# Two thirds of a modulation product: from the first stage into prompt attention

## The chip, the cores and the metric

One core of a Trainium2 chip runs the whole program. The time is device microseconds of one execution; the figure of a kernel is the median over its runs. "The trace" is one profiled execution of the kernel before, with a start and a duration for every instruction and transfer, counted in microseconds from the start of its span.

Engines are named as the profile names them: PE multiplies matrices, PEld loads its weights, DVE and ACT are the vector and the scalar engine, POOL is GpSimd, SP only issues transfers. A line such as "SPq" is the instruction queue of SP.

## The reference, cut to what matters

```python
def _decoder_layer(x, c, conv_prefix, attend, layer_idx, p):
    shift1, scale1, gate1, shift2, scale2, gate2 = _adaln(c, p['w_ada'], p['b_ada'])  # silu(c) @ w_ada + b_ada
    h = x * (1 + scale1) + shift1
    proj = h @ p['w_in']                       # q, k, v, B, C, u
    ...
    o_att = _diff_post(attend(q, k, v, lam), p['subln_w'], lam_init)
    o_conv, conv_state = _short_conv(gb, gc, hc, conv_prefix, p['conv_w'])
    mix = jnp.concatenate([o_att, o_conv], axis=-1) @ p['w_out']
    x = _layer_norm(DEEPNORM_ALPHA * x + gate1 * mix, p['ln1_g'], p['ln1_b'])
    h2 = x * (1 + scale2) + shift2
    f = _peer(h2.reshape(b * s, d), ...).reshape(b, s, d)
    x = _layer_norm(DEEPNORM_ALPHA * x + gate2 * f, p['ln2_g'], p['ln2_b'])
```

The layer runs for a prompt (1024 tokens, one row of c) and for a sample group (8 sequences of 4 tokens, eight rows of c) with the same weights. `w_ada` is 1024 x 6144 floats, 25 MB: six vectors of 1024 for each of the nine rows of c. `shift1` and `scale1` are wanted by the projection; `gate1`, `shift2`, `scale2` and `gate2` only after attention.

## The kernel before

`build` runs six stages one after another, each closed by a barrier of all engines (`end_stage`): `condition` (modulation, bias tables), `project` (q, k, v, then `conv`), `prompt_attention`, `sample_attention` (paged cache), `mix` (output product, first layer norm) and `peer` (expert retrieval, 1056 indirect gathers, by far the longest).

**condition.** SP loads `w_ada` in 12 blocks of 512 columns (2 MB each, L201) into four slots, then the three parts of `w_qkv` that the next stage multiplies (2 MB each, L204). PE multiplies each block as it lands: 32 matmuls with 128 columns (L257), each of which the trace shows as two instructions, so 64 for a block. After four blocks DVE adds the bias (L303) into `mod`. The first four blocks are shift1 and scale1; they alone are turned into `modT`. When all twelve are done, SP stores `mod` to DRAM with four transfers (`mod_scratch`, L207), waits for them (L208) and for `w_qkv` (L209). `mix` reads the last four vectors from that scratch.

**prompt_attention.** There are 32 units k, eight tiles t of 128 queries by four heads h; unit k has (k // 4 + 1) * 128 keys. `heads` sets one fixed order on each engine: in turn k PE does `scores` of unit k+3 (L665), `turn` of unit k+1 (transposes of the weights, L673) and `values` of unit k (L682); DVE does `combined` of unit k+1 (L709 to L716) and `biased` of unit k+3 (bias and row maximum, L698 to L702); ACT does the exponentials of unit k+2 (L730), the copy of the turned weights of unit k+1 (L737) and, after the last head of a tile, the copy of the output (L744). The scores have one set of PSUM banks: `scores` of the next unit waits until `biased` has read the last. The output banks alternate by tile (6 and 7). SP loads the four bias strips (576 KB each, L641), for all of which DVE waits before its first unit, and then issues the 18 stores of the convolution's state (L645, L647), 512 elements of 4 bytes each, and waits for them before the barrier.

Of the kernel before, what the change touches and what calls it, by code (L numbers as in the profile page):

```python
# [99 lines left out]
def build(nc, A):  # L100
    with ExitStack() as top:
# [28 lines left out]
        with ExitStack() as mid:  # L130
            pre = ExitStack()
            tensors |= dict(pre=pre, w_qkv=sbuf(pre, "w_qkv", [P, KD, 3 * AW], side="right"))
            tensors["modT"] = sbuf(mid, "modT", [P, 2, KD, NC])
            condition(**tensors)
# [20 lines left out]
def condition(nc, A, sem, sbuf, psum, mod_dram, toep_dram, ident, ones, modT, lam, eps, w_qkv, **_):  # L155

    NBLK, SL, G = 12, 4, 4  # L160
    with ExitStack() as st:
        w = sbuf(st, "w_ada", [P, SL, KD, BANK])
# [4 lines left out]
        cT = sbuf(st, "cT", [P, KD, NS])  # L167
        lq = sbuf(st, "lq", [1, 4, DH])
# [9 lines left out]
        consts, b_land, b_zero = sem("consts"), sem("b_ada_land"), sem("b_ada_zero")  # L178
        w_land, w_free = ([sem(f"w_ada_{what}{u}") for u in range(SL)] for what in ("land", "free"))
        qkv_land, mod_first = sem("w_qkv_land"), sem("mod_first")  # L180
        silu, cT_psum, cT_sbuf = sem("silu"), sem("cT_psum"), sem("cT_sbuf")
        m_psum, m_free = [sem(f"m_psum{u}") for u in range(2)], [sem(f"m_free{u}") for u in range(2)]
        mod_ready, modT_psum, lam_exp, lam_arg, lam_bc, lam_row = (sem("mod_ready"), sem("modT_psum"), sem("lam_exp"),
                                                                  sem("lam_arg"), sem("lam_bc"), sem("lam_row"))
        dve_c, act_c, ones_ready, mod_stored = sem("dve_c"), sem("act_c"), sem("ones_ready"), sem("mod_stored")
# [3 lines left out]
        mod_v = mod_dram.rearrange("c (n j x) -> c n j x", j=G, x=P)  # L189
        with nc.Block() as block:  # L190
            @block.sync
            def _(sp):
                sp.dma_start(rel[0:BUCKETS, :], A["rel_bias"]).then_inc(rel_land, 16)
                sp.dma_start(hot[:], A["const_onehot"]).then_inc(rel_land, 16)
                sp.dma_start(c[0:1, :], A["c_prompt"]).then_inc(consts, 16)
                sp.dma_start(c[1:NC, :], A["c_sample"]).then_inc(consts, 16)
                sp.dma_start(ident[:], A["const_ident"]).then_inc(consts, 16)
                for n in range(NBLK):
                    if n >= SL:
                        sp.wait_ge(w_free[n % SL], n // SL)  # L200
                    sp.dma_start(w[:, n % SL], w_v[:, :, n * BANK:(n + 1) * BANK]).then_inc(w_land[n % SL], 16)  # L201
                for j in range(3):
                    cols = slice(j * AW, (j + 1) * AW)
                    sp.dma_start(w_qkv[:, :, cols], wq_v[:, :, cols]).then_inc(qkv_land, 16)  # L204
                sp.wait_ge(mod_ready, 1)
                for j in range(G):
                    sp.dma_start(mod_v[:, :, j, :], mod[j * NS:j * NS + NC]).then_inc(mod_stored, 16)  # L207
                sp.wait_ge(mod_stored, 16 * G)  # L208
                sp.wait_ge(qkv_land, 16 * 3)  # L209

            @block.scalar
            def _(act):
# [3 lines left out]
                for j in range(G):  # L216
                    act.dma_start(b4[j * NS:j * NS + NC], b_v[:, :, j, :].to_broadcast([NC, NBLK, P])).then_inc(b_land, 16)
                act.wait_ge(consts, 7 * 16)
# [11 lines left out]
            def _(pe):  # L230
# [18 lines left out]
                for n in range(NBLK):  # L249
                    u, m, at = n % SL, (n // G) % 2, (n % G) * P  # L250
                    pe.wait_ge(w_land[u], 16 * (n // SL + 1))
                    if n == 2 * G:
                        pe.wait_ge(m_free[m], 1)
                    for k in range(KD):
                        for j in range(G):

                            ins = nc.tensor.matmul(psum[j * NS:(j + 1) * NS, m, at:at + P], cT[:, k, :], w[:, u, k, j * P:(j + 1) * P],  # L257
                                                   start=(k == 0), stop=(k == KD - 1), skip_group_check=True)
                    ins.then_inc(w_free[u], 1)
                    if n % G == G - 1:  # L260

                        pe.wait_ge(w_free[u], n // SL + 1)
                        pe.sem_inc(m_psum[m], 1)

# [8 lines left out]
            def _(dve):  # L273
# [26 lines left out]
                dve.wait_ge(b_land, 16 * G)  # L300
                for q in range(NBLK // G):
                    dve.wait_ge(m_psum[q % 2], q // 2 + 1)
                    step(nc.vector.tensor_tensor(mod[:, q * G:(q + 1) * G, :].rearrange("p n x -> p (n x)"), psum[:, q % 2, :],  # L303
                                                 b4[:, q * G:(q + 1) * G, :].rearrange("p n x -> p (n x)"), ALU.add))
                    step.tell(m_free[q % 2], *([mod_first] if q == 0 else []))
                step.tell(mod_ready)
                dve.wait_ge(modT_psum, 1)
# [300 lines left out]

def prompt_attention(nc, A, sem, sbuf, psum, toep_dram, ident, ones, lam, qT, kT, v, o_att, zlast, zslast, **_):

# [4 lines left out]
    with ExitStack() as st:  # L615
# [5 lines left out]
        mx, nmx, z = (sbuf(st, n, [P, 3, 2]) for n in ("row_max", "neg_max", "row_sum"))  # L621
        rz = sbuf(st, "row_scale", [P, 2])
        T = {n: sem("at_" + n) for n in
             "s_ready s_free e_ready p_ready w_ready w_free wT_psum wT_free wT_ready o_ready o_free".split()}
        dve_c, act_c, strip_land, state_stored = sem("at_dve"), sem("at_act"), sem("at_strip"), sem("at_state_stored")

        def heads(*parts):


            for k in range(-3, TILES * H):  # L630
                for ahead, part in parts:
                    if 0 <= k + ahead < TILES * H:
                        part(k + ahead, (k + ahead) // H, (k + ahead) % H)

        with nc.Block() as block:
            @block.sync
            def _(sp):
                for h in range(H):

                    f = toep_dram[h].rearrange("q m -> (q m)")[P - 1:P - 1 + P * (TOEP - 1)]  # L640
                    sp.dma_start(strip[:, h, :], f.rearrange("(q m) -> q m", q=P)[:, 0:STRIP]).then_inc(strip_land, 16)  # L641

                with nc.allow_non_contiguous_dma("small"):
                    for r in range(2):
# [4 lines left out]
                sp.wait_ge(state_stored, 16 * 2 * (1 + NB))  # L649

            @block.tensor
            def _(pe):
                pe.sem_inc(T["s_free"], 1)
                pe.sem_inc(T["w_free"], 1)
                pe.sem_inc(T["wT_free"], 1)
                pe.sem_inc(T["o_free"], 2)

# [31 lines left out]
            def _(dve):  # L689
# [15 lines left out]
                def combined(k, t, h):  # L705
# [13 lines left out]
                    step.reset()  # L719
                heads((1, combined), (3, biased))  # L720

            @block.scalar
            def _(act):
# [17 lines left out]
                def output(k, t, h):  # L741
                    if h == H - 1:
                        take(act, T["o_ready"])
                        step(nc.scalar.copy(o_att[:, t, :], psum[:, 6 + t % 2, :]))  # L744
                        step.tell(T["o_free"])
                        step.reset()
# [1202 lines left out]
```

## Time and profile before

| | us |
|---|---|
| median of 3 runs | 3984.93 |
| lowest and highest of the 3 | 3982.57, 3989.07 |
| the profiled execution | 3991.51 |
| its span in the trace | 3989.5 |
| first stage, in the trace | 0 to about 95 |
| prompt attention, in the trace | about 480 to 649 |

The page of the profile gives for the whole span PE 60% busy, DVE 64%, ACT 37%, POOL 33%, and the DMA engines at nine tenths or more in 29 of the 40 slices, most of them in `peer`. Since the stages are closed by barriers, a stage's length is set by whatever ends last inside it, and its rows have to be read by themselves.

### The profile page before, as it was taken

How to read it: one execution, taken by the hardware profiler on the slowest of the kernel's cores; microseconds unless marked ns; L12 is line 12 of the kernel's file. 1: busy time of each engine (PE TensorE's matmuls, PEld its weight loads, DVE VectorE, ACT ScalarE, POOL GpSimd, SP SyncE). 2: the span in 40 equal slices, each digit the busy share in tenths (PEclk: the TensorE clock that was granted, in tenths of full speed). 3: DMA queues.
4: the chain of work that ended last, by engine and by line, in shares of the span. 5: the costliest groups of instructions: out<-in, count | busy, mean ns of one | idle time of the engine just before them, and what ended most of it. 6: DMA issues, size and time to landing. Idle time of an engine off the chain costs nothing. (4 is left out here: it accounts for less than half of the span.)

```text
span 3989.5 us, 55293 instructions
## 1 busy us (share of the span) xinstructions
PE 2409.4 (60%) x16678; PEld 1084.2 (27%) x16678; DVE 2542.6 (64%) x6416; ACT 1465.6 (37%) x4223; POOL 1296.8 (33%) x1334
## 2 busy tenths in 40 slices
PE   5999776898765354553564465465356456446543
PEld 3446445565322121220121121122112112112110
DVE  1111165666475888677677677767757767767775
ACT  0110053333003455543434444444444344444443
POOL 0000001444002344443444344444344444444442
PEclk7999978999887565775675676566567567657655
DMA  9102134999328899999999999999999999999998
GB/s 359 49 33 61 24 1 144 407 411 387 138 92 315 353 396 404 421 420 421 411 417 413 419 415 418 403 421 412 421 407 418 419 406 420 421 420 414 419 412 333
DMA packets 245932, 1343.89 MB, mean 337 GB/s; under 512 B 47288, under 2 KB 60825, under 8 KB 94084
## 3 DMA queue, kind: packets, MB, share of 16 engines
q0 software_dynamic: 164352, 1174.49, 71.4%
q1 hardware_dynamic: 64072, 147.14, 10.9%
q10 hardware_dynamic: 17212, 18.74, 1.4%
q8 instruction: 133, 2.18, 0.2%
q14 instruction: 163, 1.34, 0.1%
HBM read 1319.30 MB, written 20.97 MB: 336 GB/s over the span
## 5 line engine op out<-in xcount | busy, mean ns | idle before, releaser
L1595 PE MATMUL psum<-sb_ring,sb_fold_weighted 128*32 128x256 f32 x8448 | 1008.9, 569 | 1307.6 <-PEq L62 1203.0
L1563 POOL DMA_INDIRECT sb_ring<-in_uv,sb_experts x1056 | 1151.4, 1090 | 1655.6 <-POOLq L62 1504.6
L1780 DVE CUSTOM_DVE_ANT_0 sb_ring<-sb_ring,sb_h_four 128x1024 f32<-128x1024 f32 x1056 | 1265.8, 1225 | 652.6 <-DMA sb_ring<-in_uv,sb_experts 615.4
L1595 PEld LDWEIGHTS psum<-sb_ring,sb_fold_weighted 128*32 128x32 f32 x8448 | 268.6, 134 | 2012.8 <-issue 2003.2
L1685 ACT ACTIVATE sb_gelu<-sb_dots 128x1 f32<-128x1 f32 x1056 | 210.3, 199 | 994.4 <-ACTq L62 985.8
L806 POOL DMA_DIRECT2D sb_v_pages<-in_cache_v x256 | 135.0, 527 | 861.5 <-issue 683.5
L1690 ACT ACTIVATE sb_fold_weighted<-sb_fold,sb_expert_w 128x32 f32<-128x32 f32 x1056 | 339.3, 321 | 34.4
L1618 PE MATMUL psum<-sb_w_pq,sb_h2T 128*128 128x512 f32 x576 | 336.6, 738 | 1.5 <-issue 1.5
L1687 ACT ACTIVATE sb_expert_w<-sb_gelu,sb_gates 128x1 f32<-128x1 f32 x1056 | 311.1, 295 | 34.5
L1664 ACT COPY sb_h_four<-sb_h_tiles 32x1024 f32<-32x1024 f32 x180 | 187.5, 1042 | 4.2
L1618 PEld LDWEIGHTS psum<-sb_w_pq,sb_h2T 128*128 128x128 f32 x576 | 132.4, 242 | 193.4 <-issue 193.4
L541 PE MATMUL psum<-sb_hT,sb_w_bcu 128*128 128x352 f32 x576 | 172.3, 462 | 8.4 <-PEq L62 8.4
L386 PE MATMUL psum<-sb_w_qkv,sb_hT_tile 128*128 128x512 f32 x384 | 168.0, 597 | 0.0
L849 PE MATMUL psum<-sb_ident,sb_k_pages 128*128 128x128 f32 x1024 | 127.6, 279 | 42.3 <-DMA sb_k_pages<-in_cache_k 24.9
L849 PEld LDWEIGHTS psum<-sb_ident,sb_k_pages 128*128 128x128 f32 x1024 | 113.7, 143 | 58.5 <-DMA sb_k_pages<-in_cache_k 37.8
L541 PEld LDWEIGHTS psum<-sb_hT,sb_w_bcu 128*128 128x128 f32 x576 | 110.3, 192 | 69.9 <-issue 9.7
L950 ACT COPY sb_k_pagesT<-psum 128x512 f32<-128x512 f32 x128 | 74.2, 587 | 107.3 <-PE psum L849 104.1
L1030 DVE COPY sb_k_pagesT<-psum 128x512 f32<-128x512 f32 x128 | 86.1, 689 | 43.0 <-PE psum L849 39.5
L466 DVE TENSOR_SCALAR sb_hT_tile<-psum,sb_modT 128x128 f32<-128x128 f32 x64 | 21.1, 405 | 135.7 <-DVEq L62 135.7
L1734 ACT COPY sb_queries<-psum 128x512 f32<-128x512 f32 x36 | 21.1, 586 | 208.9 <-ACTq L62 208.9
L386 PEld LDWEIGHTS psum<-sb_w_qkv,sb_hT_tile 128*128 128x128 f32 x384 | 73.1, 192 | 89.2 <-issue 89.1
L1793 DVE MAX8 sb_sv<-sb_scores_pk 128x8 f32<-128x128 f32 x288 | 69.9, 285 | 32.1 <-DVEq L62 29.5
(227 smaller groups left out, 2646.7 us busy)
## 6 DMA issues: line engine op xcount, KB each, us to landing
sb_k_pages<-in_cache_k SPq DMA_DIRECT2D x256, 256.0 KB, 6.1
sb_v_pages<-in_cache_v POOLq DMA_DIRECT2D x256, 256.0 KB, 6.2
sb_w_ada<-in_w_ada SPq DMA_DIRECT2D x12, 2048.0 KB, 17.0
sb_ring<-in_uv,sb_experts POOLq DMA_INDIRECT x1056
sb_w_qkv<-in_w_in SPq DMA_DIRECT2D x3, 2048.0 KB, 19.3
sb_w_bcu<-in_w_in SPq DMA_DIRECT2D x12, 512.0 KB, 6.3
sb_w_pq<-in_w_pq SPq DMA_DIRECT2D x3, 2048.0 KB, 17.1
sb_h_tiles<-h_scratch SPq DMA_DIRECT2D x9, 512.0 KB, 9.2
```

The source lines that it names most:

```text
L386: ins = nc.tensor.matmul(psum[0:n, 2 + j, :], hTt[:, u, k, 0:n], w[:, k, j * AW:(j + 1) * AW], start=(k == 0), stop=(k == KD - 1))
L541: ins = nc.tensor.matmul(where(u, part, j), w[:, u, j, k, :], hT[:, k, at:at + n], start=(k == 0), stop=(k == KD - 1))
L806: eng.dma_start(slots[g::CH, u, :, :].rearrange("q j n -> q (j n)"), cache[ds(page, 1)].rearrange("a (q j) n -> (a q) (j n)", j=CH))\
L849: ins = nc.tensor.transpose(psum[:, KT + h, j * P:(j + 1) * P], kp[:, u, j, h * P:(h + 1) * P], ident[:])
L1563: pool.indirect_dma_start(ring[:, slot, :], None, uv, bass.IndirectOffsetOnAxis(ap=experts[:, u, g, n:n + 1], axis=0))\
L1595: ins = nc.tensor.matmul(psum[q * NS:(q + 1) * NS, bank, at:at + QUARTER], fw[:, slot, :], ring[:, slot, D + q * QUARTER:D + (q + 1) * QUA ...
L1618: ins = nc.tensor.matmul(psum[:, 4 + n % 2, :], hT[:, k, :], w[:, k, n * BANK:(n + 1) * BANK], start=(k == 0), stop=(k == KD - 1), skip_gr ...
L1664: step(nc.scalar.copy(h2x[q * NS:(q + 1) * NS, half, :], h2[g * NS:(g + 1) * NS, u, :]))
L1685: step(nc.scalar.activation(act_g[:, slot:slot + 1], dots[:, slot:slot + 1], ACT.Gelu))
L1687: step(nc.scalar.activation(wgt[:, slot:slot + 1], act_g[:, slot:slot + 1], ACT.Copy, scale=gates[:, u, g, n:n + 1]))
L1690: nc.scalar.activation(fw[:, slot, :], fold[:, 0:NS], ACT.Copy, scale=wgt[:, slot:slot + 1]).then_inc(T["diag_ready"], 1)
L1780: dot = nc.vector.tensor_tensor_reduce(ring[:, slot, 0:D], ring[:, slot, 0:D], h2x[:, half], 1.0, 0.0, ALU.mult, ALU.add, dots[:, slot:slo ...
```

## The change

Blocks 4 to 11 of `w_ada` leave `condition`. In `prompt_attention` they come back as 16 pieces of 1 MB (half the depth of a block, two slots), loaded by SP behind the strips and the bias rows, and multiplied by PE behind `values` in turns 2 to 9 and 12 to 19, with 16 matmuls a piece. DVE adds each pile of four blocks to the bias in turns 10 and 20. The store to `mod_scratch` now stands in this stage, and the state stores stand behind it in SP's queue. PE's product takes PSUM bank 7, so the output banks no longer alternate. `cT` moves to a buffer that lives longer. POOL clears the 128 x 1024 tile `mod_late` before SP loads the bias rows into it.

```diff
@@ condition
-    NBLK, SL, G = 12, 4, 4
+    NBLK, G = 4, 4
...
                 for n in range(NBLK):
-                    if n >= SL:
-                        sp.wait_ge(w_free[n % SL], n // SL)
-                    sp.dma_start(w[:, n % SL], w_v[:, :, n * BANK:(n + 1) * BANK]).then_inc(w_land[n % SL], 16)
+                    sp.dma_start(w[:, n], w_v[:, :, n * BANK:(n + 1) * BANK]).then_inc(w_land[n], 16)
...
-                sp.wait_ge(mod_ready, 1)
-                for j in range(G):
-                    sp.dma_start(mod_v[:, :, j, :], mod[j * NS:j * NS + NC]).then_inc(mod_stored, 16)
-                sp.wait_ge(mod_stored, 16 * G)
                 sp.wait_ge(qkv_land, 16 * 3)
@@ prompt_attention
+        w_ada = sbuf(st, "w_ada_late", [P, 2, HALF, BANK])
+        mod = sbuf(st, "mod_late", [P, NBLK, P])
...
+        OUT, MOD = 6, 7
+        def modulation(k):
+            if 2 <= k < 2 + NBLK:
+                return k - 2
+            if 12 <= k < 12 + NBLK:
+                return k - 12 + NBLK
+            return None
@@ block.sync, behind the four strips
+                sp.wait_ge(mod_zero, 1)
+                for j in range(G):
+                    sp.dma_start(mod[j * NS:j * NS + NC], b_v[:, G:G + NBLK, j, :].to_broadcast([NC, NBLK, P])).then_inc(b_land, 16)
+                for i in range(2 * NBLK):
+                    u, n, half = i % 2, i // 2, i % 2
+                    if i >= 2:
+                        sp.wait_ge(w_free[u], n)
+                    sp.dma_start(w_ada[:, u], w_v[:, half * HALF:(half + 1) * HALF, (G + n) * BANK:(G + n + 1) * BANK]).then_inc(w_land[u], 16)
+                sp.wait_ge(mod_ready, PILES)
+                for j in range(G):
+                    sp.dma_start(mod_v[:, G:G + NBLK, j, :], mod[j * NS:j * NS + NC]).then_inc(mod_stored, 16)
+                sp.wait_ge(mod_stored, 16 * G)
                 with nc.allow_non_contiguous_dma("small"):
@@ block.tensor
-                        ins = nc.tensor.matmul(psum[:, 6 + t % 2, h * DV:(h + 1) * DV], wT[:, k % 2, j, :],
+                        ins = nc.tensor.matmul(psum[:, OUT, h * DV:(h + 1) * DV], wT[:, k % 2, j, :],
...
+                def modulate(k, t, h):
+                    i = modulation(k)
+                    if i is None:
+                        return
+                    u, n, half = i % 2, i // 2, i % 2
+                    if i == NBLK:
+                        pe.wait_ge(mod_ready, 1)
+                    pe.wait_ge(w_land[u], 16 * (n + 1))
+                    for c in range(HALF):
+                        for g in range(G):
+                            ins = nc.tensor.matmul(psum[g * NS:(g + 1) * NS, MOD, n % G * P:(n % G + 1) * P], cT[:, half * HALF + c, :],
+                                                   w_ada[:, u, c, g * P:(g + 1) * P], ...)
+                    ins.then_inc(w_free[u], 1)
+                    if (i + 1) % NBLK == 0:
+                        pe.wait_ge(w_free[u], n + 1)
+                        pe.sem_inc(m_psum, 1)
-                heads((3, scores), (1, turn), (0, values))
+                heads((3, scores), (1, turn), (0, values), (0, modulate))
@@ block.vector
+                def modulated(k, t, h):
+                    if k not in (10, 20):
+                        return
+                    pile = (k - 10) // 10
+                    dve.wait_ge(m_psum, pile + 1)
+                    dve.wait_ge(b_land, 16 * G)
+                    part = mod[:, pile * G:(pile + 1) * G, :].rearrange("p n x -> p (n x)")
+                    step(nc.vector.tensor_tensor(part, psum[:, MOD, :], part, ALU.add))
+                    step.tell(mod_ready)
-                heads((1, combined), (3, biased))
+                heads((1, combined), (3, biased), (0, modulated))
```

The order on SP in the first stage and in prompt attention, before (`x12` and the like count transfers of one form; `sb_z_last` and `sb_z_sample_last` are the convolution's state):

```order
L201 DMA sb_w_ada<-in_w_ada 128x8x512 x12
L204 DMA sb_w_qkv<-in_w_in 128x8x512 x3
L207 DMA mod_scratch<-sb_mod 108x1x128 x4
...
L641 DMA sb_bias_strip<-toep_scratch 128x1152 x4
L645 DMA out_new_conv_prompt<-sb_z_last 128x4x1
L647 DMA out_new_conv_sample<-sb_z_sample_last 128x4x1 x8
```

and with the change:

```order
L198 DMA sb_w_ada<-in_w_ada 128x8x512 x4
L201 DMA sb_w_qkv<-in_w_in 128x8x512 x3
...
L644 DMA sb_bias_strip<-toep_scratch 128x1152 x4
L648 DMA sb_mod_late<-in_b_ada 9x8x128 x4
L653 DMA sb_w_ada_late<-in_w_ada 128x4x512 x16
L656 DMA mod_scratch<-sb_mod_late 9x8x128 x4
L660 DMA out_new_conv_prompt<-sb_z_last 128x4x1
```

Eight blocks and the store of `mod` have gone from the first stage, and 24 transfers stand between the strips and the first state store.

The order on PE in prompt attention, turns 2 and 3 without the `scores` that open turn 2, before:

```order
L673 MATMUL psum<-sb_ident,sb_weights 128x128
L682 MATMUL psum<-sb_v,sb_weightsT 128x128
L665 MATMUL psum<-sb_kT,sb_qT 128x256 x2
L673 MATMUL psum<-sb_ident,sb_weights 128x128 x2
L682 MATMUL psum<-sb_v,sb_weightsT 128x128
```

and with the change:

```order
L692 MATMUL psum<-sb_ident,sb_weights 128x128
L701 MATMUL psum<-sb_v,sb_weightsT 128x128
L716 MATMUL psum<-sb_w_ada_late,sb_cT 32x128 x16
L684 MATMUL psum<-sb_kT,sb_qT 128x256 x2
L692 MATMUL psum<-sb_ident,sb_weights 128x128 x2
L701 MATMUL psum<-sb_v,sb_weightsT 128x128
L716 MATMUL psum<-sb_w_ada_late,sb_cT 32x128 x16
```

A piece of 16 matmuls, and the wait for its landing ahead of it, now stands between `values` and the next `scores`.

## Rows read from the trace of the kernel before

**Rows 1.** Engines' busy time by stretch, first stage: columns in the first line.
```profile
core 0: us, PE busy (x) PEld busy (x) DVE busy (x) ACT busy (x) POOL busy (x), PEclk, DMA share, GB/s
0.00:95.00 95.00, 53.34 (x806) 38.03 (x806) 11.47 (x23) 4.05 (x5) 0.20 (x4) 0.79 0.98 367
```

**Rows 2.** Timeline of PE, `w_ada` blocks: start, duration, what, [idle before, its releaser].
```profile
36.14 3.64 PE L257 MATMUL psum<-sb_w_ada,sb_cT 128*32 128x128 f32 x64 [2.91 <-DMA sb_w_ada<-in_w_ada]
...
46.38 1.95 PE L257 MATMUL psum<-sb_w_ada,sb_cT 128*32 128x128 f32 x64 [1.49 <-DMA sb_w_ada<-in_w_ada]
...
77.14 1.95 PE L257 MATMUL psum<-sb_w_ada,sb_cT 128*32 128x128 f32 x64 [2.02 <-DMA sb_w_ada<-in_w_ada]
```

**Rows 3.** End of the first stage: SP's issues, then SP's waits (total, times, longest).
```profile
80.14 7.13 SPq L207 DMA_DIRECT2D mod_scratch<-sb_mod  x4
95.77 0.99 SPq L355 DMA_DIRECT2D sb_x_in<-in_x_prompt  x2
...
SPq L209 <- DMA sb_w_qkv<-in_w_in: 6.0, 1, 6.0
...
SPq L190 <- DMA mod_scratch<-sb_mod: 1.0, 1, 1.0
```

**Rows 4.** Start of prompt attention: timeline, the strips' landing, then stretches (columns of rows 1).
```profile
480.47 2.13 SPq L641 DMA_DIRECT2D sb_bias_strip<-toep_scratch  x4
...
483.12 18.59 SPq L647 DMA_DIRECT2D out_new_conv_sample<-sb_z_sample_last  x8
499.02 0.29 DVE L698 CUSTOM_DVE_ANT_0 sb_scores<-psum,sb_bias_strip 128x128 f32<-128x128 f32 x1 [19.76 <-DVEq L62]
...
DMA to landing us min/median/max: 3.8/6.0/16.7
...
480.00:490.00 10.00, 0.80 (x4) 0.54 (x4) 0.00 (x0) 0.00 (x0) 0.00 (x0) 0.50 0.79 237
490.00:499.00 9.00, 0.00 (x0) 0.00 (x0) 0.00 (x0) 0.00 (x0) 0.00 (x0) 0.50 0.52 1
```

**Rows 5.** Issue to landing of the 512 KB loads of `w_bcu`, issued in threes.
```profile
DMA to landing us min/median/max: 3.9/6.3/9.3
```

**Rows 6.** Timeline of PE, one turn with 384 keys at the low clock.
```profile
528.73 1.65 PE L665 MATMUL psum<-sb_kT,sb_qT 64*128 64x384 f32 x4 [0.65 <-PEq L62]
...
530.75 0.88 PE L673 MATMUL psum<-sb_ident,sb_weights 128*128 128x128 f32 x3 [0.37 <-PEq L62]
...
531.42 1.06 PE L682 MATMUL psum<-sb_v,sb_weightsT 128*128 128x128 f32 x4
...
532.41 1.65 PE L665 MATMUL psum<-sb_kT,sb_qT 64*128 64x384 f32 x4
```

**Rows 7.** Timeline of PE, one turn with 512 keys at the high clock.
```profile
543.76 1.13 PE L665 MATMUL psum<-sb_kT,sb_qT 64*128 64x512 f32 x4 [0.68 <-PEq L62]
...
545.98 0.63 PE L673 MATMUL psum<-sb_ident,sb_weights 128*128 128x128 f32 x4 [1.09 <-PEq L62]
...
546.45 0.83 PE L682 MATMUL psum<-sb_v,sb_weightsT 128*128 128x128 f32 x6
...
547.85 1.13 PE L665 MATMUL psum<-sb_kT,sb_qT 64*128 64x512 f32 x4 [0.57 <-PEq L62]
```

**Rows 8.** PE alone, a stretch of early units: length, busy, granted clock, DMA share, GB/s.
```profile
509.00:519.00 10.00, 7.32 (x26) 0.50 1.43 2
```

**Rows 9.** Timeline of DVE: the addition of a pile of four blocks.
```profile
40.02 0.69 DVE L303 TENSOR_TENSOR sb_mod<-psum,sb_b_ada 128x512 f32<-128x512 f32 x1 [12.68 <-PEq L263]
```

**Rows 10.** State stores' last issues and SP's wait; end of DVE's turn 20; last output copy.
```profile
503.43 16.70 SPq L647 DMA_DIRECT2D out_new_conv_sample<-sb_z_sample_last  x8
...
SPq L635 <- DMA out_new_conv_sample<-sb_z_sample_last: 16.1, 1, 16.1
...
589.92 0.17 DVE L702 TENSOR_SCALAR sb_neg_max<-sb_row_max 128x2 f32<-128x2 f32 x1
...
647.80 0.59 ACT L744 COPY sb_o_att<-psum 128x512 f32<-128x512 f32 x1 [2.49 <-ACTq L62]
```

More of the change, by code:

```diff
@@ L133, in build @@
             tensors["modT"] = sbuf(mid, "modT", [P, 2, KD, NC])
+            tensors["cT"] = sbuf(mid, "cT", [P, KD, NS])
             condition(**tensors)
@@ L152, in build, with condition @@
         peer(**tensors)
-def condition(nc, A, sem, sbuf, psum, mod_dram, toep_dram, ident, ones, modT, lam, eps, w_qkv, **_):
-    NBLK, SL, G = 12, 4, 4
+def condition(nc, A, sem, sbuf, psum, toep_dram, ident, ones, modT, cT, lam, eps, w_qkv, **_):
+    NBLK, G = 4, 4
     with ExitStack() as st:
-        w = sbuf(st, "w_ada", [P, SL, KD, BANK])
+        w = sbuf(st, "w_ada", [P, NBLK, KD, BANK])
         b4 = sbuf(st, "b_ada", [P, NBLK, P])
@@ L178, in condition @@
         consts, b_land, b_zero = sem("consts"), sem("b_ada_land"), sem("b_ada_zero")
-        w_land, w_free = ([sem(f"w_ada_{what}{u}") for u in range(SL)] for what in ("land", "free"))
+        w_land = [sem(f"w_ada_land{n}") for n in range(NBLK)]
         qkv_land, mod_first = sem("w_qkv_land"), sem("mod_first")
         silu, cT_psum, cT_sbuf = sem("silu"), sem("cT_psum"), sem("cT_sbuf")
-        m_psum, m_free = [sem(f"m_psum{u}") for u in range(2)], [sem(f"m_free{u}") for u in range(2)]
-        mod_ready, modT_psum, lam_exp, lam_arg, lam_bc, lam_row = (sem("mod_ready"), sem("modT_psum"), sem("lam_exp"),
+        m_psum = sem("m_psum")
+        modT_psum, lam_exp, lam_arg, lam_bc, lam_row = (sem("modT_psum"), sem("lam_exp"),
                                                                   sem("lam_arg"), sem("lam_bc"), sem("lam_row"))
-        dve_c, act_c, ones_ready, mod_stored = sem("dve_c"), sem("act_c"), sem("ones_ready"), sem("mod_stored")
+        dve_c, act_c, ones_ready = sem("dve_c"), sem("act_c"), sem("ones_ready")
         w_v = A["w_ada"][0].rearrange("(k p) n -> p k n", p=P)
@@ L249, in _ @@
                 for n in range(NBLK):
[L250 to L253, printed above, removed]
+                    pe.wait_ge(w_land[n], 16)
                     for k in range(KD):
                         for j in range(G):
-                            ins = nc.tensor.matmul(psum[j * NS:(j + 1) * NS, m, at:at + P], cT[:, k, :], w[:, u, k, j * P:(j + 1) * P],
+                            ins = nc.tensor.matmul(psum[j * NS:(j + 1) * NS, 0, n * P:(n + 1) * P], cT[:, k, :], w[:, n, k, j * P:(j + 1) * P],
                                                    start=(k == 0), stop=(k == KD - 1), skip_group_check=True)
[L259 to L263, printed above, removed]
+                ins.then_inc(m_psum, 1)
                 pe.wait_ge(mod_first, 1)
@@ L300, in _ @@
                 dve.wait_ge(b_land, 16 * G)
[L301 to L306, printed above, removed]
+                dve.wait_ge(m_psum, 1)
+                step(nc.vector.tensor_tensor(mod[:].rearrange("p n x -> p (n x)"), psum[:, 0, :], b4[:].rearrange("p n x -> p (n x)"), ALU.add))
+                step.tell(mod_first)
                 dve.wait_ge(modT_psum, 1)
@@ L606, in _, with prompt_attention @@
                 blocks(dve, body)
[L609 removed]
+def prompt_attention(nc, A, sem, sbuf, psum, toep_dram, ident, ones, lam, qT, kT, v, o_att, zlast, zslast, cT, mod_dram, **_):
     with ExitStack() as st:
@@ L622, in prompt_attention @@
         rz = sbuf(st, "row_scale", [P, 2])
+        G, HALF, PILES = 4, KD // 2, 2
+        NBLK = PILES * G
+        w_ada = sbuf(st, "w_ada_late", [P, 2, HALF, BANK])
+        mod = sbuf(st, "mod_late", [P, NBLK, P])
+        mod_zero, b_land, m_psum, mod_ready, mod_stored = (sem("at_" + n) for n in "mod_zero b_land m_psum mod_ready mod_stored".split())
+        w_land, w_free = ([sem(f"at_w_ada_{what}{u}") for u in range(2)] for what in ("land", "free"))
+        w_v = A["w_ada"][0].rearrange("(k p) n -> p k n", p=P)
+        b_v = A["b_ada"].rearrange("a (n j x) -> a n j x", j=G, x=P)
+        mod_v = mod_dram.rearrange("c (n j x) -> c n j x", j=G, x=P)
+        OUT, MOD = 6, 7
[5 more added lines that the diff above has]
+            return None
         T = {n: sem("at_" + n) for n in
@@ L649, in _ @@
                 sp.wait_ge(state_stored, 16 * 2 * (1 + NB))
+            @block.gpsimd
+            def _(pool):
+                nc.gpsimd.memset(mod[:], 0.0).then_inc(mod_zero, 1)
             @block.tensor
@@ L655, in _ @@
                 pe.sem_inc(T["wT_free"], 1)
-                pe.sem_inc(T["o_free"], 2)
+                pe.sem_inc(T["o_free"], 1)
                 def scores(k, t, h):
@@ L685, in values @@
                         ins.then_inc(T["o_ready"], 1)
-                heads((3, scores), (1, turn), (0, values))
+                def modulate(k, t, h):
[9 more added lines that the diff above has]
+                            ins = nc.tensor.matmul(psum[g * NS:(g + 1) * NS, MOD, n % G * P:(n % G + 1) * P], cT[:, half * HALF + c, :],
+                                                   w_ada[:, u, c, g * P:(g + 1) * P], start=(half == 0 and c == 0),
+                                                   stop=(half == 1 and c == HALF - 1), skip_group_check=True)
+                    ins.then_inc(w_free[u], 1)
[3 more added lines that the diff above has]
+                heads((3, scores), (1, turn), (0, values), (0, modulate))
             @block.vector
@@ L743, in output @@
                         take(act, T["o_ready"])
-                        step(nc.scalar.copy(o_att[:, t, :], psum[:, 6 + t % 2, :]))
+                        step(nc.scalar.copy(o_att[:, t, :], psum[:, OUT, :]))
                         step.tell(T["o_free"])
```

4 lines of the change are left out of this document (1 added, 3 removed).

## The prediction

> **What bounds the kernel now.** Most of the span is `peer`, which the change does not touch. So I read the two stages that it does touch, each by itself, since barriers close them.
>
> First the stretches. In the first 95 us the DMA engines are 0.98 busy at 367 GB/s while PE is at work for 53 us and DVE for 11 [rows 1]. The timeline of PE says the same from the other side: each block of `w_ada` is multiplied in 1.95 or 3.64 us and PE is then idle until the next lands; the ninth block from the fourth on starts at 77.14, the first of them at 36.14 [rows 2], so a 2 MB load takes (77.14 - 36.14) / 8 = 5.125 us. The stage is bound by loads. What ends it is read from SP: it issues the stores of `mod` until 80.14 + 7.13 = 87.3, waits 6.0 us for `w_qkv` and 1.0 us more for the stores, and the next stage's first load goes out at 95.77 [rows 3].
>
> Then prompt attention. The strips are issued from 480.47 on; DVE, which wants all four, starts at 499.02 [rows 4]. From there the order of turns decides. At 512 keys and the high clock a turn takes 547.85 - 543.76 = 4.09 us and PE waits twice in it: `scores` end at 544.89 and the transposes start at 545.98, `values` end at 547.28 and the next `scores` start at 547.85 [rows 7]. PE has 1.09 + 0.57 = 1.66 us of slack; DVE's chain sets the turn. At the low clock it is otherwise: in a turn of 532.41 - 528.73 = 3.68 us PE has 1.65 + 0.88 + 1.06 = 3.59 us of work [rows 6]. The last output copy ends at 648.39 [rows 10]. The stage's DMA engines carry nearly nothing after the strips.
>
> **The first stage.** Eight loads go: 8 x 5.125 = 41.0 us. The loads that stay are not slowed by it, as the queue was full all the time. The three `w_qkv` loads would then land 3 x 5.125 = 15.4 us after 36.1, at 51.5; before, they were due at 77.1 + 15.4 = 92.5 and SP saw them at 93.3, since the stores of `mod` ran among them: 0.8 us more that goes. The wait of 1.0 us for the stores goes too [rows 3]. What is late next? The fourth block is multiplied by 36.14 + 3.64 = 39.8 and its addition takes 0.69 us [rows 2, 9], so the small work behind it is done about 10 us before `w_qkv`. Sum: -42.8 us. The multiplication removed from PE here was hidden and gives nothing.
>
> **The start of attention.** All bytes of the strips (4 x 576 KB = 2.36 MB) were moved by 490: 237 GB/s over 10 us is 2.37 MB. Yet the fourth strip took 16.7 us to land where the median one took 6.0, and what ran meanwhile, at 1 GB/s and half the engines' time, were the 4-byte state stores that SP had issued right behind [rows 4]. With the change loads of 512-byte and 2 KB rows stand there instead. I take it that the strips then land by 489.5 of the old count: -9.5 us. The two ends are -10 (they land when the bytes are through) and 0 (something else held the strip). I take the near end because the median strip landed in 6.0 us.
>
> The Trainium skill speaks against this step. Its page "DMA: Bandwidth & Descriptors", section "Queues, rings and completion order", says that an engine takes descriptors in ring order and that a semaphore increment lands only after every earlier write of that engine. The state stores stand behind the strips, so by that rule they cannot have held them; the cause would be another and would stay, which gives the time of the first rival below, 3948.1 us, in place of 3938.6. The trace neither agrees nor disagrees: it shows when the bytes moved, not what the increment waited for.
>
> **The pieces on PE.** A piece is half a block: 3.64 / 2 = 1.82 us at the low clock, 1.95 / 2 = 0.98 at the high one [rows 2]. At the high clock 0.98 is less than the slack of 1.66, and less than 0.57 + 1.09 taken in their order (0.57 behind `values`, the remaining 0.41 ahead of the transposes), so the eight pieces of turns 12 to 19 cost nothing. At the low clock 1.82 us meet 0.09 of slack: 3.59 + 1.82 - 3.68 = +1.7 us a turn. The granted clock in the early turns is 0.50, at a busy share of 0.73 [rows 8]. With the pieces PE would be busy without a break from turn 2 on; in the first stage the clock rose after two blocks of 3.64 us with pauses between them [rows 2]. I expect it to rise within two or three turns: 2.5 turns, of which the first still has some slack, at 1.4: +3.5 us. The high clock then comes some 20 us sooner than now and shortens turns 5 to 9 a little: -1. Bounds: -2 to +13.6 (8 x 1.7).
>
> **The other additions.** DVE's two sums of 0.69 us [rows 9], each with its completion wait, stand on the engine that sets the turn: 2 x 1.0 = +2.0. The landing of a piece: a 2 MB load takes 5.1 us of the engines, so 1.5 MB take 3.8, and three 512 KB loads took 6.3 at the median [rows 5]; 2.5 us are thus fixed and a piece of 1 MB lands 2.56 + 2.5 = 5.1 us after its issue. A slot is freed at the end of turn k and wanted at the end of turn k+2: two turns less the piece's own product, 5.0 to 6.4 us. It just fits; where it does not, PE stands still with the next `scores` behind it, and DVE waits for those. +1, with 0 and +5 as ends. The first two pieces are issued before 486 of the old count and wanted 13 us after DVE's start: covered. POOL's clearing of `mod_late` runs beside the strips, and the 9-row bias loads are small: 0. One output bank in place of two: `values` of the next tile wait for a copy of 0.59 us that ACT does one turn earlier; covered by that turn, 0, and at most 7 x 0.6 = 4 if it is not.
>
> **The end of attention.** The state stores now start after the store of `mod`. They took from 482.6 to 503.43 + 16.70 + 16.1 = 536.2 [rows 4, 10], 53.6 us, of which some fell to the strips: 40 to 54, I take 50. DVE's turn 20 without its addition ends at 590.1, the last copy at 648.4 [rows 10]: 58.3 us are left. Against that stand the addition 1.0, four issues and the landing 5 (they took 7.1 to issue in a full queue [rows 3]) and 50: 56. It fits by 2 us; with 54 and 8 it is 5 us over. +0.5, with 0 and +5 as ends. Nothing is queued behind but the barrier, for which every engine waits.
>
> **The sum.** -42.8 - 9.5 + 3.5 - 1 + 2 + 1 + 0.5 = -46.3 us. The profiled execution (3991.5) would become 3945.2; it lies 6.6 us above the median of the runs, so I set the sum against the median: 3984.9 - 46.3 = 3938.6 us.
>
> **The rivals.**
> 1. The strips land as late as before, because something ahead of the stores held the fourth one, or because the 1 MB pieces behind it now do what the stores did. For it: no row shows which transfer held the fourth strip. Against: its landing stands out by 10 us from the others. The sum loses 9.5: 3948.1 us.
> 2. The clock stays low through turn 9, and the state stores end last. 8 x 1.7 instead of 3.5, no gain from an earlier rise, 5 at the end: -46.3 + 10.1 + 1 + 4.5 = -30.7, 3954.2 us. For it: the clock stayed at 0.50 for the early turns at a busy share of 0.73 [rows 8]. Against: PE would have no pause.
> 3. Every cost is covered, because PE's high clock comes at once: -42.8 - 9.5 = -52.3, 3932.6 us.
> 4. Slower: PE waits for the landing of each piece. With a landing of L us a turn cannot be shorter than (L + 1) / 2; the 16 turns with pieces take about 62 us now (3.7 and 4.1 us in [rows 6, 7]). The gain of 47.3 without the wait is used up when 8 x (L + 1) = 62 + 47, at L = 12.7. A fourth strip took 16.7 [rows 4]; with that, 8 x 17.7 - 62 = 80 us are lost and the time is 3984.9 - 47.3 + 80 = 4017 us. Against: the stores beside which it took so long now come after the last piece.
> 5. The change does not do what it says. The order shows the eight loads gone, so only another limit of the first stage could keep the time, and rows 1 and 2 show none.
>
> **How the numbers follow.** Forecast (3930 to 3944) 0.56; first rival 0.20, second 0.12, third 0.08, fourth 0.03, fifth 0.01. The range goes from the third rival's neighbourhood over the forecast and the first rival up to short of the second: 3930 to 3953. About 0.2 % (8 us) is what a measurement can tell from no change. All cases but the last two are faster by more: faster 0.96, same 0.01, slower 0.03.
>
> **What would show it.** The last `w_qkv` landing near 51 and the next stage's first load near 53; more than 55 breaks the first step. DVE's first unit 9 to 10 us after the first strip's issue, not 18. The first two or three pieces at 1.8 us and the rest at 1.0; a clock of 0.50 through turn 9 is the second rival. PE's idle time before a piece put down to the load of `w_ada_late`: about 1 us in all. SP's last wait ending within 5 us of the last output copy. `peer` and the stages between unchanged within 2 us. A gain under 35 us would mean that a step is wrong, not a size.

## The result

| | us | ratio to before |
|---|---|---|
| before, 4 runs | 3983.75 (3981.36 to 3989.07) | |
| changed, 4 runs | 3953.41 (3951.82 to 3957.02) | 0.9923, interval 0.9906 to 0.994 |
| forecast | 3938.6 (3930.0 to 3953.0) | |

The kernel became faster by 30 us, which is the forecast's sign, but 0.4 us above its range and 15 us above its value. The prediction had said that a gain under 35 us would mean a wrong step and not a wrong size; one step was wrong. In its trace the span is 3949.8 us. The stretches, one by one:

End of the first stage. SP's timeline (start, duration) and its wait:

```profile
14.51 20.99 SPq L201 DMA_DIRECT2D sb_w_qkv<-in_w_in  x3
51.71 105.68 SPq L338 DMA_DIRECT2D sb_x_in<-in_x_prompt  x8
...
SPq L189 <- DMA sb_w_qkv<-in_w_in: 14.8, 1, 14.8
```

SP has issued everything at 35.5 and waits 14.8 us, until 50.3, for `w_qkv`; the next stage starts at 51.71 where it did at 95.77 [rows 3]: -44.1 us.

Start of attention, the strips' issue, DVE's first unit, and the strips' landing times:

```profile
436.23 2.12 SPq L644 DMA_DIRECT2D sb_bias_strip<-toep_scratch  x4
446.93 0.29 DVE L735 CUSTOM_DVE_ANT_0 sb_scores<-psum,sb_bias_strip 128x128 f32<-128x128 f32 x1 [11.88 <-DVEq L62]
...
DMA to landing us min/median/max: 3.7/5.9/9.0
```

The slowest strip lands in 9.0 us instead of 16.7, and DVE starts 10.7 us after the issue instead of 18.55 [rows 4]: -7.9 us.

The pieces on PE, turn 2 and later ones (timeline of PE):

```profile
460.75 1.63 PE L716 MATMUL psum<-sb_w_ada_late,sb_cT 128*32 128x128 f32 x32
462.31 0.70 PE L684 MATMUL psum<-sb_kT,sb_qT 64*128 64x256 f32 x4
...
463.62 1.08 PE L716 MATMUL psum<-sb_w_ada_late,sb_cT 128*32 128x128 f32 x32
...
486.61 1.08 PE L716 MATMUL psum<-sb_w_ada_late,sb_cT 128*32 128x128 f32 x32 [0.98 <-DMA sb_w_ada_late<-in_w_ada]
```

The clock rises inside the first piece (the granted clock is 0.50 up to 461.5 and 1.00 from 462.5 on): the second takes 1.08 us, and the `scores` between them 0.70, where 1.23 was normal at the low clock. PE waits for three of the 16 pieces, 1.6 us in all, at most 0.98.

Late turns, while the state stores run (timeline):

```profile
542.62 0.40 SPq L660 DMA_DIRECT2D out_new_conv_prompt<-sb_z_last  x1
...
553.93 31.18 SPq L662 DMA_DIRECT2D out_new_conv_sample<-sb_z_sample_last  x8
...
561.76 1.09 DVE L735 CUSTOM_DVE_ANT_0 sb_scores<-psum,sb_bias_strip 128x896 f32<-128x896 f32 x1 [3.66 <-DVEq L62]
562.64 0.91 ACT L784 COPY sb_weightsT<-psum 128x896 f32<-128x896 f32 x1 [4.24 <-ACTq L62]
...
564.38 3.64 PE L684 MATMUL psum<-sb_kT,sb_qT 64*128 64x512 f32 x8 [3.41 <-DVEq L88]
...
578.10 3.15 PE L701 MATMUL psum<-sb_v,sb_weightsT 128*128 128x128 f32 x14 [3.23 <-issue]
...
604.25 0.58 ACT L791 COPY sb_o_att<-psum 128x512 f32<-128x512 f32 x1 [2.49 <-ACTq L62]
```

Here the gain is given back. DVE stands still from 558.1 and ACT from 558.4, for 3.66 and 4.24 us, with nothing that the profile names to wait for (the engine's own queue); PE's 3.41 us follow from that, since its `scores` wait for DVE. About 576 it is PE that stops, for 3.23 us ("issue"), and the other two that wait for it. I call these pauses holes. After each of them PE's next long instruction runs at the low clock (granted 0.54 and 0.50): 3.64 and 3.15 us for what takes 1.77 and 1.73. From DVE's first unit to the end of the last copy it is 157.9 us against 149.4 [rows 4, 10]. Up to unit 25 the two traces differ by 1 us; the rest of the 8.5 us comes behind it.

### The profile page after: what moved, and what is told of

Read it like the earlier page. It is cut to its first block and busy times, and to the rows that moved or that the text cites. A ratio compares the mean times of both kernels' runs of the same rounds, so it can differ in the third digit from the quotient of the medians.

```text
span 3949.8 us, 55304 instructions
## 1 busy us (share of the span) xinstructions
PE 2399.7 (61%) x16678; PEld 1075.6 (27%) x16678; DVE 2541.4 (64%) x6416; ACT 1465.4 (37%) x4223; POOL 1301.2 (33%) x1335
## 5 line engine op out<-in xcount | busy, mean ns | idle before, releaser
L896 PE MATMUL psum<-sb_ident,sb_k_pages 128*128 128x128 f32 x1024 | 127.6, 279 | 43.7 <-DMA sb_k_pages<-in_cache_k 24.9
## 6 DMA issues: line engine op xcount, KB each, us to landing
sb_ring<-in_uv,sb_experts POOLq DMA_INDIRECT x1056, 14.8
```

Of the source, the lines that this page charges most:

```text
L896: ins = nc.tensor.transpose(psum[:, KT + h, j * P:(j + 1) * P], kp[:, u, j, h * P:(h + 1) * P], ident[:])
```

## The experiments

All 11 are beside runs of the kernel before on their chip (median there 3987.0 to 3987.7). The stretches of each trace: next stage's first load; strips' issue to DVE's first unit; from there to the end of the last output copy ("attention").

| kernel | first load | strips to DVE | attention | median us | ratio (interval) |
|---|---|---|---|---|---|
| before, first trace | 95.8 | 18.5 | 149.4 | 3983.75 | |
| e1 before again | 95.3 | 15.7 | 147.1 | 3986.76 | 1.000 (0.999 to 1.0009) |
| changed, first trace | 51.7 | 10.7 | 157.9 | 3953.41 | 0.9923 (0.9906 to 0.994) |
| e2 changed again | 51.7 | 10.4 | 158.1 | 3953.04 | 0.9918 (0.9905 to 0.9932) |
| e3 states first | 51.7 | 15.4 | 179.2 | 3976.64 | 0.9973 (0.9958 to 0.9988) |
| e4 no states | 51.9 | 10.7 | 148.9 | 3941.96 | 0.9889 (0.9874 to 0.9904) |
| e5 changed, turned state | 52.4 | 10.1 | 152.0 | 3946.09 | 0.989 (0.9872 to 0.9908) |
| e6 before, turned state | 95.5 | 10.2 | 147.8 | 3983.52 | 0.999 (0.9981 to 1.0) |
| e7 one by one | 52.0 | 10.1 | 150.8 | 4055.94 | 1.0168 (1.015 to 1.0186) |
| e8 no pieces | 51.7 | 10.3 | 154.8 | 3950.54 | 0.9904 (0.9886 to 0.9922) |
| e9 turned, four slots | 51.7 | 9.8 | 148.5 | 3943.66 | 0.9891 (0.9874 to 0.9907) |
| e10 turned again | 51.9 | 10.5 | 150.2 | 3944.24 | 0.9896 (0.988 to 0.9913) |
| e11 before, strips first | 95.6 | 9.3 | 160.0 | 3991.68 | 1.0009 (1.0 to 1.0019) |

The theory was that the 4-byte stores of the convolution's state hold up whatever else wants a DMA engine, in the old place the strip's landing, in the new one the late turns. Rivals: the holes belong to the pieces, DVE's additions or the single output bank; the strip was held by something ahead of it.

**e1 and e2, both kernels again** (no edit).

> The kernel before, unchanged, for a second trace. Between the two traces the first stage and prompt attention became 43.5 us shorter up to the last output copy and the span 39.7, but the medians of the runs differ by only 30.3. Theory A: the one trace of before was a long execution (3991.5 against a median of 3983.8) and its excess lies in the long last stage. Then this trace has a span near 3981, the next stage's first load again at 95.8 +/- 0.5, DVE's first unit 18 to 19 us after the strips' issue and the last output copy at 648 +/- 2. Rival: prompt attention itself varies from run to run; then the last copy moves by 5 us or more.

> The changed kernel, unchanged, in five rounds. In the first trace prompt attention from DVE's first unit to the last copy took 157.3 us against 148.8 before, and the 8.5 us appear in two holes behind unit 25 and unit 28, while the 4-byte state stores run. Theory A: these holes belong to the state stores and come in every execution, though not in the same turns: 5 to 12 us longer than before again, all of it between the issue of the first state store and the landing of the last. Rival: they were an accident of that execution, and attention takes 149 to 152 us here. The ratio of the times should be 0.991 to 0.993.

The span of e1 is 3985.0, where about 3981 was expected, and DVE starts 15.7 us after the issue, where 18 to 19 were expected; attention is 147.1 us and the last copy ends at 643.4, 5 us earlier, as the rival had it. So how long the stores held the strips differs between executions, 5 us here instead of 8, and the excess of the first trace was partly there. The changed kernel repeats its attention to 0.2 us, holes in the same turns included: they are no accident. From e1 to e2 the stretches change by -43.7 (first stage), -5.3 (strips), +11.0 (attention) and +1.3 for the rest (-1.4 between the first stage and attention, +2.7 behind attention): -36.7 us of span; the medians beside each other differ by 33.7.

**e3, the 18 state stores back behind the strips.**

```diff
                     sp.dma_start(strip[:, h, :], ...).then_inc(strip_land, 16)
+                with nc.allow_non_contiguous_dma("small"):
+                    ...
                 sp.wait_ge(mod_zero, 1)
```

> The changed kernel with the 18 state stores put back right behind the strips, ahead of the bias rows and the pieces. Theory A (the 4-byte stores hold up whatever else wants a DMA engine: the strip's landing, and the fetch of the engines' instructions): DVE's first unit again comes 16 to 20 us after the strips' issue instead of 10.7, the holes in the last turns are gone, and the pieces wait instead, because SP issues them only behind the stores: PE stands still at its first pieces for some 15 to 35 us. In all 5 to 25 us slower than the change. Rival 1 (the fourth strip was held by something ahead of it in the queue): DVE's first unit stays where the change has it. Rival 2 (the holes come from the pieces, the addition or the single output bank): the holes stay in the last turns.

```profile
451.99 0.29 DVE L735 CUSTOM_DVE_ANT_0 sb_scores<-psum,sb_bias_strip 128x128 f32<-128x128 f32 x1 [16.59 <-DVEq L62]
...
494.66 1.93 PE L716 MATMUL psum<-sb_w_ada_late,sb_cT 128*32 128x128 f32 x32 [28.79 <-DMA sb_w_ada_late<-in_w_ada]
```

DVE's first unit is late again (15.4 us after the issue, 16 to 20 expected), and PE stands 28.79 us before its first piece, because the pieces queue behind the stores. The holes in the last turns are gone: from DVE's unit 24 to its unit 31 it takes 39.5 us, as in e4 below, against 47.2 with the change, although the pieces, the additions and the single output bank are all still there. Expected 5 to 25 us slower than the change: 23.6.

**e4, no state stores** (left out with their wait).

> The changed kernel without its 18 state stores and without the wait for them; the two outputs of the convolution's state are not written. Theory A: no hole in the last turns, attention from DVE's first unit to the last copy takes 149 to 152 us, the stage ends with the last copy, and the time is 8 to 12 us below the change. DVE's first unit stays at 10.7 us after the strips' issue, since nothing but loads stands behind the strips in either. Rival: the holes stay, the time moves by less than 3 us.

```profile
557.69 1.09 DVE L728 CUSTOM_DVE_ANT_0 sb_scores<-psum,sb_bias_strip 128x896 f32<-128x896 f32 x1 [0.41 <-DVEq L62]
...
558.77 0.91 ACT L777 COPY sb_weightsT<-psum 128x896 f32<-128x896 f32 x1 [1.19 <-ACTq L62]
```

These are the two instructions ahead of which DVE and ACT stood 3.66 and 4.24 us with the change. Attention is 148.9 us and the time 11 us below the change: as expected, and the rivals of the holes fall. The profile's table of DMA queues shows what lay beside. The changed kernel from 555 to 580:

```profile
q8 instruction: 1, 0.02, 2.2%
q14 instruction: 1, 0.01, 1.6%
```

and e4 from 540 to 560 (columns: packets, MB, share of 16 engines' time):

```profile
q8 instruction: 1, 0.02, 0.3%
q14 instruction: 2, 0.02, 0.2%
```

One packet of the instruction queue q8 took 0.022 x 16 x 25 = 8.8 us beside the stores and 0.003 x 16 x 20 = 1.0 without; one of q14 6.4 us against 0.3. That the engines stood still for want of those packets is a possible link, not a shown one: the profile does not tell for which instruction a packet was, and the times do not fit well. The slow packet of q14 ran from 558.8 to 565.1, while DVE was at work again at 561.8; that of q8 ran from 564.9 to 573.7 and was through before PE stopped at 574.9. What is shown is that the holes come and go with the queued stores; how the stores stop the engines stays open.

**e5 and e6, the state turned.** PE transposes the 8 and 64 columns of the state before its first scores, DVE copies them while it would wait for the strips, and SP stores rows of 128 floats.

```diff
+                nc.tensor.transpose(psum[0:2 * H, 7, 0:P], zlast[:].rearrange("p h r -> p (h r)"), ident[:])
+                nc.tensor.transpose(psum[0:2 * H * NB, 7, P:2 * P], zslast[:].rearrange("p h b r -> p (h b r)"), ident[:]).then_inc(st_psum, 1)
...
+                for h in range(H):
+                    cols = slice(h * P, (h + 1) * P)
+                    sp.dma_start(A["new_conv_prompt"][0, 0][:, cols], rows[2 * h:2 * (h + 1), 0, :]).then_inc(state_stored, 16)
+                    sp.dma_start(A["new_conv_sample"][0][:, :, cols].rearrange("b r p -> (b r) p"), rows[2 * NB * h:2 * NB * (h + 1), 1, :]).then_inc(state_stored, 16)
```

> The changed kernel with the convolution's state turned by two transposes on PE while DVE still waits for the strips, so that it is stored in eight transfers of 512-byte rows instead of 18 of single floats; all outputs are written. Theory A (the cost lies in the thousands of 4-byte writes): as without the stores, within 2 us: attention from DVE's first unit 149 to 151 us, strips to DVE 10 to 11 us, 10 to 12 us below the change, so 3941 to 3944. Rival (any HBM store that late or that early holds the strips or the stage): less than half of that.

> The kernel before with the same turned state, all outputs written. It prices what the 4-byte stores cost in their old place. Theory A: DVE's first unit comes 8 to 10 us after the strips' issue instead of 15.7 to 18.5, and attention shortens by 0 to 3 us (one fetch of instructions was slow there too): 6 to 11 us below before. Rival 1 (the fourth strip was held by something ahead of it): no change of DVE's first unit, less than 3 us in all.

e5 is 7 us below the change, with all outputs written; 10 to 12 were expected, and less than half of that by the rival. Its attention is 3 us longer than e4's, and one piece came late:

```profile
477.37 1.49 PE L722 MATMUL psum<-sb_w_ada_late,sb_cT 128*32 128x128 f32 x32 [2.33 <-DMA sb_w_ada_late<-in_w_ada]
...
DMA to landing us min/median/max: 5.0/5.3/9.5
```

In the kernel before, the same edit brings DVE's first unit to 10.2 us as expected, but the time falls by 3.7 us only (0 to 7.6), where 6 to 11 were expected. A later stage accounts for some of it: from the load of `w_out` to the first gather e5, e6, e9 and e10 take 228.3 to 229.3 us and the others with a trace there 225.5 to 227.5. Whether the turned state lengthens it, and why, is open.

**e7, one store at a time.**

```diff
                             sp.dma_start(A["new_conv_sample"][0, b, r].rearrange("(c p) -> p c", p=P), zslast[:, :, b, r]).then_inc(state_stored, 16)
+                            sp.wait_ge(state_stored, 16 * (r * (1 + NB) + b + 2))
```

> The changed kernel where SP waits for each of the 18 state stores before it issues the next, so that never more than one transfer of 512 floats is queued. Theory A with a queue as its mechanism (the fetch of instructions waits behind what is already queued on its engine): the holes shrink to under 3 us in all and attention takes 150 to 153 us, while the stores take as long as now or up to 20 us longer and may end last. Rival (the writes as such slow every access, queued or not): the holes stay at 7 us or more.

```profile
SPq L663 <- DMA out_new_conv_sample<-sb_z_sample_last: 128.6, 14, 10.5
...
596.83 0.58 ACT L793 COPY sb_o_att<-psum 128x512 f32<-128x512 f32 x1 [2.49 <-ACTq L62]
713.14 0.27 SPq L862 DMA_DIRECT2D sb_page_table<-in_page_table  x1
```

The holes are gone (attention 150.8 us), so a single store in flight does no visible harm; it takes many of them queued together. e7 also spreads the writes over some 170 us in place of 57, so it does not tell the length of the queue from the rate of the writes. The other half of the expectation failed: a single store of 512 floats takes about 9 us to land (128.6 / 14 = 9.2 us of waiting each), 18 of them run 115 us past the last copy, and the kernel is 103 us slower than the change.

**e8, no pieces.** Late load, product and additions are left out; the last four modulation vectors are the bias alone.

```diff
-                for i in range(2 * NBLK):
-                    ...
-                sp.wait_ge(mod_ready, PILES)
+                sp.wait_ge(b_land, 16 * G)
-                heads((3, scores), (1, turn), (0, values), (0, modulate))
+                heads((3, scores), (1, turn), (0, values))
```

> The changed kernel without the late product: no late load of the weight, no product and no addition, the last four modulation vectors are the bias alone; the bias rows and their store stay, and the state stores follow them early in attention, as in the kernel before. It prices the pieces and the first stage apart. Theory A: the first stage as with the change (next load at 51.7), DVE's first unit 11 to 18 us after the strips' issue, attention 147 to 150 us, the time 40 to 47 us below before. Set against the change without stores (attention 148.9 us), the pieces then cost 0 to 2 us in attention. Rival (the pieces are what makes attention longer): attention here is 5 us or more shorter than in the change without stores.

The first stage and the strips are as with the change, so neither gain needs the pieces. DVE starts 10.3 us after the strips' issue (11 to 18 expected), the time is 36.7 us below before (40 to 47 expected), and attention is 154.8 us, longer than the 147 to 150 expected: the stores now start at 451.4, after DVE has begun, and there is a hole in the early turns instead. So this run cannot price the pieces; the comparison with e6 below does.

```profile
487.11 1.65 PE L679 MATMUL psum<-sb_kT,sb_qT 64*128 64x384 f32 x4 [6.14 <-PEq L62]
```

**e9 and e10, four slots and two.**

```diff
-        w_ada = sbuf(st, "w_ada_late", [P, 2, HALF, BANK])
+        SLOTS = 4
+        w_ada = sbuf(st, "w_ada_late", [P, SLOTS, HALF, BANK])
...
-                    u, n, half = i % 2, i // 2, i % 2
-                    if i >= 2:
-                        sp.wait_ge(w_free[u], n)
+                    u, n, half = i % SLOTS, i // 2, i % 2
+                    if i >= SLOTS:
+                        sp.wait_ge(w_free[u], i // SLOTS)
```

> The changed kernel with the turned state and four slots for the late pieces in place of two, all outputs written. With two slots and the turned state one piece landed 9.5 us after its issue in place of 5.3 at the median, and PE stood still for 2.3 us before it. Theory A: with four slots no piece is waited for (under 0.3 us in all), attention from DVE's first unit takes 148.5 to 150 us, and the time is 1 to 4 us below the turned state with two slots, near 3942. Rival (that late piece was rare and the slots don't matter): no difference beyond noise, 3944 to 3947.

> The changed kernel with the turned state and two slots once more, beside the one with four slots, for an interval. Theory A: 3943 to 3947, 6 to 11 us below the change, attention 149 to 152 us, strips to DVE 10 to 11 us. If the late piece of the first trace was an accident, PE waits less than 1 us for pieces here; if two slots are too few for it, some piece again lands 8 us or more after its issue.

With four slots no piece is waited for and attention is 148.5 us; with two it is 150.2, one piece again lands 9.5 us after its issue, and PE waits 1.9 us for three pieces. So the late piece of e5 was no accident. In the time nothing of that can be told: 3943.66 and 3944.24 are the same. Against e6 (147.8 us, no pieces at all) the pieces, their waits and DVE's two additions cost 0.7 to 2.4 us (e9, e10).

**e11, the kernel before with the stores held until the strips have landed.**

```diff
+                sp.wait_ge(strip_land, 16 * H)
                 with nc.allow_non_contiguous_dma("small"):
```

> The kernel before, where SP waits for the strips to land before it issues the state stores; nothing else is changed. It takes the stores from behind the strips and nothing else. Theory A (the 4-byte stores behind the strips hold the fourth strip's landing): DVE's first unit comes 10 to 10.7 us after the strips' issue in place of 15.7 and 18.5, the stores then fall on the first turns and stretch them, attention takes 150 to 156 us in place of 147 to 149, and the time is within 6 us of before. Rival (something ahead of the strips held it): DVE's first unit stays at 15 us or more.

```profile
480.63 2.13 SPq L641 DMA_DIRECT2D sb_bias_strip<-toep_scratch  x4
489.75 0.40 SPq L646 DMA_DIRECT2D out_new_conv_prompt<-sb_z_last  x1
489.93 0.29 DVE L699 CUSTOM_DVE_ANT_0 sb_scores<-psum,sb_bias_strip 128x128 f32<-128x128 f32 x1 [10.52 <-DVEq L62]
...
512.25 1.23 PE L666 MATMUL psum<-sb_kT,sb_qT 64*128 64x256 f32 x4 [8.42 <-PEq L62]
```

DVE starts after 9.3 us: the stores behind the strips did hold them. What they held was not the data. In e1, with the stores behind, the last of the strips' 512 packets ended at 489.5, the last strip counted as landed only 13.9 us after its issue, and DVE started at 496.3; in e11 that packet ended at 489.4, the strip landed after 7.6 us, and DVE started at 489.9. (In the first trace one packet of 512 took 5.3 us and ended at 495.3.)

And the stores then open a hole of 8.42 us in the first turns; attention is 160.0 us, more than the 150 to 156 expected, and the time 4.6 us above before, within the 6 expected. From the strips' issue to the last copy, the sum of two columns of the table, e6 with the turned state takes 158.0 us, the kernel before 162.8 and 167.9, and e11 169.3. So the same stores cost 5 to 10 us in their old place, most of it in the wait for the strips, and 11 beside the first turns.

## Why the prediction failed, step by step

- **The first stage**, -42.8 forecast, -44.1 and (e1 to e2) -43.7 measured. Right: the loads bounded it, 5.125 us each, and `w_qkv` was next.
- **The strips**, -9.5 forecast, -7.9 and -5.3 measured. Right in mechanism (e3, e6 and e11), too large in size: the value before is not one number (18.5 and 15.7), and 10.7 to 10.4 remain instead of 9.0. The rule of the Trainium skill's page "DMA: Bandwidth & Descriptors" (section "Queues, rings and completion order"), read as I read it, gave the first rival; e11 disagrees with that reading: with the stores behind them the strips take until 15.7 or 18.5, without them until 9.3. The measurement decides. The rule says behind what an increment has to come, and I took it to say that nothing else can delay it; e1 and e11 show the increment late while the data was not.
- **The pieces**, +3.5 and -1 for PE, +2 for DVE, +1 for landings, 5.5 in all; 0.7 to 2.4 measured. The clock rose within the first piece, not after 2.5 turns. My rows for it were thin: between the three blocks shown in [rows 2] the clock of the first stage fell and rose again (the nine blocks took 3.64, 3.64, 1.95, 3.10, 3.64, 3.64, 1.96, 3.12 and 1.95 us). The landing of a piece was 5.1 us by my estimate and 5.2 to 5.3 at the median of e5, e9 and e10.
- **The end of attention** is the step that failed. I asked only whether the state stores would end before the last copy and priced that at +0.5. They took 56.7 us (542.6 to 585.1 and 14.2 of wait), 50 forecast, and did end in time. But I priced nothing for what they do to the turns beside which they run. That is +9.1 us (158.0 in the two traces against 148.9 in e4) and 11 in the medians. The trace of before already held a hint: while the stores ran, DVE stood 1.70 us ahead of one of its units, where the same pause was 0.41 in the turn before and in e1:

```profile
519.64 0.42 DVE L698 CUSTOM_DVE_ANT_0 sb_scores<-psum,sb_bias_strip 128x256 f32<-128x256 f32 x1 [1.70 <-issue]
```

  I took the 18 us wait for the strips as the stores' whole harm, and did not ask what their new neighbours would be.
- **Two errors that partly cancel.** For attention as a whole I forecast +6.0 us; +8.5 and (e1 to e2) +11.0 were measured. The harm of the stores was missing with 9.1 us, and the pieces were priced 3 to 5 us too high. Without that luck the forecast would have missed by more.
- **The rivals.** The measured 3953.4 lies beside the second rival's 3954.2, by chance: the clock did not stay low, and the state stores ended at 599.3, before the last copy at 604.8. In the fourth rival the 62 us for sixteen turns were too low; in the trace of before they take 67.8, which makes its time 4011 instead of 4017.
- **The sum.** Measured by trace: -44.1 - 7.9 + 8.5 = -43.5 up to the last copy, and -39.7 for the span; +3.8 us came behind the last copy, and +2.7 from e1 to e2. That remainder, from the last copy to the end, runs from 3340.8 us (e4) to 3349.0 (e9) over the traces, so I cannot put it down to the change. The medians differ by 30.3 in the first comparison and 33.7 in the second. So some 3 to 9 us lie between what one pair of traces says and what the medians say; a single profiled execution of this kernel (before: 3981.0 to 3993.7 over 16 runs) does not fix a sum to better than that.
- Without the state stores the change gives 3942.0 (e4), 3.4 us from the forecast and 45.8 below the runs of before beside it, where -46.3 was forecast. That this is so near is in part luck too: the strips gave less than forecast and the pieces cost less.

## What to carry to other kernels

When a transfer of many tiny elements is moved in a queue, price it twice: its own duration, and what it does to everything beside it in the new place. Here the same 18 stores cost 5 to 10 us by the traces while DVE waited for the strips anyway (3.7 in the medians of e6), 9 us in the late turns and 11 in the first ones. Turning the data on an idle engine so that rows are stored is better than either place that they had in these two kernels: 3944 to 3946 us with every output written, against 3953 for the change and 3987 for the kernel before.

## What was not expected of the hardware

A store of 512 single floats to DRAM, alone in its queue, took about 9.2 us to land, while a 1 MB load took 5.2 to 5.3. Such stores, queued behind a load, delayed the count of its landing by 6 us (13.9 against 7.6 from issue) though its last packet ended at the same time (489.5 and 489.4). And with 18 of them in the queue one packet of an instruction queue took 8.8 us where it takes 1.0 otherwise, and two engines paused for 3.7 and 4.2 us at about the same moment; that the one caused the other is not shown.
